# Expert products in unsplit fp32 on four 32-column groups of TensorE, instead of three split products on the whole array

## The chip, the core and the metric

The kernel runs on one core of a Trainium2 chip. The metric is the device time of one execution in microseconds (us). Below, PE is TensorE, ACT is ScalarE, DVE is VectorE, POOL is GpSimd and SP is SyncE, whose queue issues the weight loads.

## The reference

The program is a two-layer trunk for 256 tokens of 1024 numbers. Layer 0 is a gated mixer and a dense SwiGLU, layer 1 a gated recurrence (HGRN2) and a SwiGLU over experts. The change is in the experts:

```python
def swiglu(h, w_gu, w_down):
    gate, up = jnp.split(h @ w_gu, 2, axis=-1)
    return (jax.nn.silu(gate) * up) @ w_down

def moe_swiglu(h, w_router, b_router, w_gu, w_down):
    logits = (h @ w_router).astype(jnp.float32) + b_router.astype(jnp.float32)
    top_logit, top_idx = lax.top_k(logits, TOP_K)
    top_w = jax.nn.softmax(top_logit, axis=-1)
    gates = jnp.sum(jax.nn.one_hot(top_idx, N_EXPERTS, dtype=jnp.float32) * top_w[..., None], axis=-2)
    out = jnp.zeros_like(h)
    for e in range(N_EXPERTS):
        out = out + gates[..., e:e + 1] * swiglu(h, w_gu[e], w_down[e])
    return out
```

There are 8 experts, each token goes to 2 of them, and the inner width of an expert is 3584. All weights are fp32: 1024 x 7168 and 3584 x 1024 for each expert, 44 MB. For the inputs of this case the router sends 56, 64, 68, 53, 55, 73, 59 and 84 tokens to the eight experts.

## The kernel before

**Split products.** Every large product is made of three: a weight block W is split into `w_hi` (ACT, line 1075, a copy with rounding to fp32r) and `w_lo` (DVE, line 1487, W minus `w_hi`), the tokens likewise, and `split_matmul` (lines 508 to 510) adds hi x hi, lo x hi and hi x lo into one PSUM bank. A product takes 128 tokens as the stationary operand and 512 weight columns as the moving one.

**Weights.** They come in granules of 1 MB (128 partitions x 2048), each in two halves of 512 KB. A load lands in one of six places (three in `raw`, three in `SC`, which are free in the expert phase). ACT and DVE turn each half into a place of the rings `w_hi` and `w_lo`, six granules deep. SP waits for `lo_done` (DVE is done with the half) before it loads the place again, ACT waits for `used` (PE is done) before it fills a ring place again.

**The expert phase.** Work comes in items. An item is one expert with up to 128 of its tokens; an expert with more would get a further item. With the counts above there are 8 items. An item has seven units of 512 hidden columns. In a unit `unit_gu` makes the gate (`side` 0, bank 0) and the up part (`side` 1, bank 1), each 8 steps over the 1024 inputs, ACT applies silu (line 1375), DVE multiplies (line 1991), `unit_turn` transposes the 128 x 512 result in four pieces (line 963), ACT and DVE split it into `hT_hi` and `hT_lo`, and `unit_down` multiplies it with the down weights into banks 4 and 5, 8 steps. The order on PE is: gate and up of unit u+1, down of unit u, turn of unit u+1. A step below is one such piece of 128 inputs by 512 weight columns; a unit has 24 of them, an item 168, the phase 1344.

**Around an item.** The rows of the next expert's tokens are fetched by an indirect DMA (line 486), transposed by `turn_xg` (line 927) and split into `xT_hi`, `xT_lo`; an item's result is copied to `yo` (line 1383) and written to its tokens' rows by another indirect DMA (line 479). `turn_rows` (line 935) makes the row numbers. The last item isn't written out but stays as `ye` and is added with a selecting product (`scatter`, line 1047). The table of items is made by DVE (`tables`), in the middle of item 0. After the experts come the last norm and the gated embedding, again with split weights.

**Small fp32 products elsewhere.** Layer 1 has products that stay in fp32: `level` (lines 782 to 803) makes attention blocks whose stationary operand has 32 columns and whose output goes to PSUM partitions 0, 32, 64 and 96 in turn (line 794: only two of the four; line 787: 64 columns, one place).

Of the kernel before, what the change touches and what calls it, by code (L numbers as in the profile page):

```python
# [31 lines left out]
P = 128  # L32
# [11 lines left out]
def trunk(nc, x_d, pT_d, columns_d, norm_g, w_in_ab, a_ln_g, a_ln_b, wsT_d, w_out_ab, ffn_w_gu,  # L44
# [12 lines left out]
    XTRA = T * P * 2 // (P + 1)  # L57
# [15 lines left out]
    with ExitStack() as ctx:  # L73
# [15 lines left out]
        hT_lo = sb("hT_lo", [P, N], F32R)  # L89
        SC = sb("SC", [P, 9 * 1024 + 8])  # L90
# [19 lines left out]
        tab = sb("tab", [P, 2, T, ITEMS + 2])  # L110
        selT = sb("selT", [P, T, P])
# [33 lines left out]
        hh = junk[:, :].bitcast(F32)[:, N:2 * N]  # L145

# [29 lines left out]
        row = spare[:, 0:T * (ITEMS + 2)].rearrange("p (t j) -> p t j", t=T)  # L176
        dst = spare[:, 64:65].bitcast(I32)
# [8 lines left out]
        ye = raw[:, 0, 0:D].rearrange("p (k c) -> p k c", c=P)  # L186
# [41 lines left out]
        gat_done, xg_act, xg_ready = sem("gathered"), sem("xg_act"), sem("xg_ready")  # L228
        ye_act, sc_done, acc_done = sem("ye_act"), sem("scattered"), sem("acc_done")
# [64 lines left out]
        def _(sp):  # L294
            def load(g, src, turns=0, first=False):

                back = RAW if g < G_MOE or first else RING
                for s in range(2):
                    part = slice(s * HW, (s + 1) * HW)
                    if g >= RAW:  # L300
                        sp.wait_ge(lo_done, turns * 2 * RING + (2 * (g - back) + s + 1))
                    sp.dma_start(raw_part(g, s), src[:, part]).then_inc(raw_full[raw_slot(g)][s], 16)
# [61 lines left out]
            def unit_down(g, e, u, turns):  # L364
                for j in range(2):
                    src = dn[bass.ds(e, 1), bass.ds(u * (N * D) + j * 256 * D, 256 * D)]
                    load(g + j, src.rearrange("e (p m) -> p (e m)", p=P), turns)
# [35 lines left out]
        def _(pool):  # L403
# [37 lines left out]
            for n, v in enumerate(gains):  # L441
# [6 lines left out]
                pool.dma_start(gain[:, :], v.broadcast_to([P, D])).then_inc(gain_full, 16)  # L448
# [26 lines left out]
            def write_rows(i):  # L475
# [3 lines left out]
                pool.indirect_dma_start(ybuf[:, :], bass.IndirectOffsetOnAxis(ap=dst, axis=0), yo,  # L479
                                        None).then_inc(rows_written, 16)  # L480

            def fetch_rows(i):
# [3 lines left out]
                pool.indirect_dma_start(xg_rows, None, xbuf[:, :], bass.IndirectOffsetOnAxis(ap=origin, axis=0)).then_inc(x_rows, 16)  # L486
# [13 lines left out]
            pool.dma_start(xn[:, :, :], ybuf[SEQ:ROWS, :].rearrange("(t p) n -> p t n", p=P)).then_inc(y_loaded, 16)  # L500
            for t in range(T):
                root_y(3, t)
# [3 lines left out]
        def _(pe):  # L506
# [402 lines left out]
            def gather(quarter):  # L909

                for k in (2 * quarter, 2 * quarter + 1):
                    for t in range(T):
                        m = pe.matmul(PS[:, GATHERED[quarter], (k % 2) * P:(k % 2 + 1) * P], xn[:, t, k * P:(k + 1) * P],  # L913
                                      sel[:, t, :], start=(t == 0), stop=(t == T - 1), skip_group_check=True)
                m.then_inc(gat_done, 1)

            def turn_sel():
                for t in range(T):
                    m = pe.matmul(PS[:, 3, t * P:(t + 1) * P], sel16[:, t, :], ident16[:, :], start=True, stop=True,
# [3 lines left out]
            def turn_xg(n):  # L923

                pe.wait_ge(x_rows, n * 16)
                for k in range(KT):
                    m = pe.transpose(PS[:, 6 + k // HK, (k % HK) * P:(k % HK + 1) * P], xg_rows[:, k * P:(k + 1) * P], ident[:, :])  # L927
# [3 lines left out]
            def turn_rows():  # L931

                for t in range(T):
                    for a in range(2):
                        m = pe.matmul(PS[:, 3, 0:2], sel16[:, t, :], pick[:, t, a, :], start=(t == 0 and a == 0),
                                      stop=(t == T - 1 and a == 1), skip_group_check=True)
                m.then_inc(rows_psum, 1)

            def unit_gu(g, turns, tokens=None, sides=(0, 1), quarters=False):

                for side in sides:
                    for h in range(2):
                        if tokens is not None and side == 0:
                            pe.wait_ge(xg_ready, tokens + (h - 1))
                        for j in range(HK):
                            if quarters and j % 2 == 0:
                                pe.wait_ge(xg_ready, 2 * h + j // 2 + 1)
# [6 lines left out]
                            if j % 2:  # L954
                                m.then_inc(used, 1)

            def unit_turn(n):
                pe.wait_ge(h_ready, n)
                hv = hh.rearrange("p (j q r) -> p j r q", j=2, r=2)
                for j in range(2):  # L960
                    for r in range(2):
                        c = (j * 2 + r) * P
                        m = pe.transpose(PS[:, 2, c:c + P], hv[:, j, r, :], ident[:, :])  # L963
                m.then_inc(hT_psum, 1)

            def unit_down(g, n, last, turns, first=False):
                pe.wait_ge(hT_ready, n)
                for j in range(2):
                    for r in range(2):
                        pe.wait_ge(lo_done, turns * 2 * RING + (2 * (g + j) + r + 1))  # L970
                        for c in range(2):
                            a = slice((j * 2 + r) * P, (j * 2 + r + 1) * P)
                            w = slice(r * D + c * N, r * D + (c + 1) * N)
                            s = (g + j) % RING
                            m = split_matmul(PS[:, 4 + c, :], hT_hi[:, a], hT_lo[:, a],
# [1219 lines left out]
```

## Time and profile before

| | us |
|---|---|
| median of 3 runs (lowest to highest) | 1452.75 (1451.99 to 1452.84) |
| the profiled execution | 1452.55 |
| its span, first to last instruction | 1450.8 |

The span is 1.75 us shorter than the profiled execution's own time. An instruction's line is that of the helper that emits it, so the split products of all stages share lines 508 to 510, and the expert phase is found by its place in time.

### The profile page before, as it was taken

What the parts mean: (1) busy time and instruction counts of PE and PEld (TensorE: products, weight loads), DVE (VectorE), ACT (ScalarE), POOL (GpSimd) and SP (SyncE); (2) the same over time, 40 slices, a digit from 0 to 9 for tenths busy, and PEclk for the clock granted to TensorE, in tenths of its full rate; (3) what the DMA queues carried; (4) which work ended last, traced back from release to release, by engine and by line L of the source; (5) the groups of instructions that cost most, each with busy time, mean ns of one, the idle gap of its engine ahead of it and who ended that gap; (6) DMA issues with size and microseconds to landing.
All of it is one profiled execution on the core that took longest, in us unless ns stands there. A gap on an engine that the chain in (4) does not pass through costs nothing.

```text
span 1450.8 us, 24554 instructions
## 1 busy us (share of the span) xinstructions
PE 1440.7 (99%) x7475; PEld 1193.4 (82%) x7475; DVE 1215.0 (84%) x1439; ACT 1006.8 (69%) x1250; POOL 55.7 (4%) x60
## 2 busy tenths in 40 slices
PE   9999999999999999999999999999999999999998
PEld 6888888888787888888888888888888888888886
DVE  7986545567897999998898899999899989989985
ACT  7565444366357888777877787777787787778773
POOL 1010000000001300000000000000000000000000
PEclk9999999999999999999999999999999999999999
DMA  8577555466255999999999999999999989999960
GB/s 309 180 251 238 192 198 178 150 197 230 80 175 205 411 410 370 381 410 391 323 412 410 349 370 409 353 372 410 375 338 411 409 324 399 410 351 397 410 266 30
DMA packets 124786, 452.73 MB, mean 312 GB/s; under 512 B 14000, under 2 KB 14000, under 8 KB 124736
## 3 DMA queue, kind: packets, MB, share of 16 engines
q1 hardware_dynamic: 119952, 435.21, 79.7%
q0 software_dynamic: 4640, 16.82, 3.3%
q8 instruction: 31, 0.51, 0.1%
q14 instruction: 19, 0.16, 0.0%
q10 hardware_dynamic: 144, 0.03, 0.0%
HBM read 443.62 MB, written 8.39 MB: 312 GB/s over the span
## 4 chain that ended last, share of the span: by engine, by line
PE 97%; DVE 2%; issue 0%; DMA 0%; ACT 0%; SPq 0%; DVEq 0%
PE PS L508 30%; PE PS L510 30%; PE PS L509 30%; PE PS L963 2%; DVE w_lo L1487 1%; PE PS L559 1%; DMA raw<-in_w_in_ab 0%; PE PS L803 0%; PE PS L927 0%; PE PS L649 0%; PE PS L913 0%; PE PS L893 0%; PE PS L851 0%; PE PS L1047 0%; PE PS L769 0%
## 5 line engine op out<-in xcount | busy, mean ns | idle before, releaser
L1487 DVE TENSOR_TENSOR w_lo<-raw,w_hi 128x1024 fp32r<-128x1024 f32 x486 | 568.5, 1219 | 32.9 <-ACT w_hi L1075 30.5
L508 PE MATMUL PS<-w_hi,xT_hi 128*128 128x512 f32 x1432 | 567.7, 396 | 0.6 <-DVE w_lo L1487 0.6
L510 PE MATMUL PS<-w_lo,xT_hi 128*128 128x512 f32 x1432 | 558.2, 390 | 0.0
L509 PE MATMUL PS<-w_hi,xT_lo 128*128 128x512 f32 x1432 | 557.2, 389 | 0.0
L1075 ACT ACTIVATE w_hi<-raw 128x1024 fp32r<-128x1024 f32 x486 | 490.2, 1061 | 59.6 <-PE PS L510 38.1
L1487 DVE TENSOR_TENSOR w_lo<-SC,w_hi 128x1024 fp32r<-128x1024 f32 x340 | 392.1, 1218 | 8.0 <-ACT w_hi L1075 6.5
L1075 ACT ACTIVATE w_hi<-SC 128x1024 fp32r<-128x1024 f32 x340 | 336.9, 1061 | 17.1 <-DMA SC<-in_e_w_gu 6.9
L510 PEld LDWEIGHTS PS<-w_lo,xT_hi 128*128 128x128 f32 x1432 | 268.8, 188 | 57.2
L508 PEld LDWEIGHTS PS<-w_hi,xT_hi 128*128 128x128 f32 x1432 | 269.7, 188 | 54.0 <-issue 1.6
L509 PEld LDWEIGHTS PS<-w_hi,xT_lo 128*128 128x128 f32 x1432 | 269.3, 188 | 53.0 <-issue 0.2
L510 PE MATMUL PS<-w_lo,hT_hi 128*128 128x512 f32 x528 | 206.1, 390 | 0.0
L508 PE MATMUL PS<-w_hi,hT_hi 128*128 128x512 f32 x528 | 205.5, 389 | 0.0
L509 PE MATMUL PS<-w_hi,hT_lo 128*128 128x512 f32 x528 | 205.4, 389 | 0.0
L510 PEld LDWEIGHTS PS<-w_lo,hT_hi 128*128 128x128 f32 x528 | 99.1, 188 | 20.6
L508 PEld LDWEIGHTS PS<-w_hi,hT_hi 128*128 128x128 f32 x528 | 99.1, 188 | 20.5
L509 PEld LDWEIGHTS PS<-w_hi,hT_lo 128*128 128x128 f32 x528 | 99.1, 188 | 20.5
L1188 ACT ACTIVATE hT_hi<-PS 128x512 fp32r<-128x512 f32 x66 | 39.8, 603 | 87.3 <-PE PS L963 58.1
L1375 ACT ACTIVATE junk<-PS 128x512 f32<-128x512 f32 x56 | 33.5, 598 | 75.2 <-PE PS L510 75.2
L1699 DVE TENSOR_TENSOR hT_lo<-PS,hT_hi 128x512 fp32r<-128x512 f32 x66 | 45.4, 687 | 42.8 <-ACT hT_hi L1188 42.7
L1991 DVE TENSOR_TENSOR junk<-junk,PS 128x512 f32<-128x512 f32 x56 | 38.2, 683 | 24.3 <-ACT junk L1375 24.3
L1693 DVE SCALAR_TENSOR_TENSOR junk<-PS,lbc,junk 128x256 f32<-128x256 f32 x22 | 9.6, 479 | 39.1 <-ACT junk L1182 39.1
L486 POOL DMA_INDIRECT SC<-xbuf,seg x7 | 13.4, 1914 | 709.0 <-DVE seg L2064 709.0
(273 smaller groups left out, 592.7 us busy)
## 6 DMA issues: line engine op xcount, KB each, us to landing
raw<-in_e_w_gu SPq DMA_DIRECT2D x226, 512.0 KB, 9.3
SC<-in_e_w_gu SPq DMA_DIRECT2D x222, 512.0 KB, 9.0
SC<-in_e_w_down SPq DMA_DIRECT2D x114, 512.0 KB, 8.1
raw<-in_e_w_down SPq DMA_DIRECT2D x110, 512.0 KB
raw<-in_ffn_w_gu SPq DMA_DIRECT2D x44, 512.0 KB, 4.9
raw<-in_w_in_c SPq DMA_DIRECT2D x32, 512.0 KB, 6.2
raw<-in_ffn_w_down SPq DMA_DIRECT2D x22, 512.0 KB, 3.9
raw<-in_w_in_ab SPq DMA_DIRECT2D x20, 512.0 KB, 6.6
```

The costliest lines, as they stand in the source:

```text
L486: pool.indirect_dma_start(xg_rows, None, xbuf[:, :], bass.IndirectOffsetOnAxis(ap=origin, axis=0)).then_inc(x_rows, 16)
L508: pe.matmul(out, a_hi, b_hi, start=start, stop=False, skip_group_check=True)
L509: pe.matmul(out, a_lo, b_hi, start=False, stop=False, skip_group_check=True)
L510: return pe.matmul(out, a_hi, b_lo, start=False, stop=stop, skip_group_check=True)
L559: m = pe.transpose(PS[:, tile_bank(t, final) + b, j * P:(j + 1) * P], src[:, t, kt * P:(kt + 1) * P], ident[:, :])
L963: m = pe.transpose(PS[:, 2, c:c + P], hv[:, j, r, :], ident[:, :])
L1075: act.activation(w_hi[:, g % RING, part], raw_part(g, s), ACT.Copy).then_inc(hi_done, 1)
L1188: act.activation(hT_hi[:, :], PS[:, b, :], ACT.Copy).then_inc(hT_act, 1)
L1375: act.activation(sg, PS[:, 0, :], ACT.Silu).then_inc(silu_done, 1)
L1487: dve.tensor_tensor(w_lo[:, g % RING, part], raw_part(g, s), w_hi[:, g % RING, part].bitcast(F32), ALU.subtract).then_inc(lo_done, 1)
L1699: dve.tensor_tensor(hT_lo[:, :], PS[:, b, :], hT_hi[:, :].bitcast(F32), ALU.subtract).then_inc(hT_ready, 1)
L1991: dve.tensor_tensor(hh, sg, PS[:, 1, :], ALU.mult).then_inc(h_ready, 1)
```

## The change

The expert phase, and nothing before it, is rewritten.

1. Its products are plain fp32 on the weights where they landed (`raw_part`). `strips` makes one step out of six products with 32 stationary columns each. The 96 tokens of an item are three groups of 32. Group k's product with weight columns 0 to 383 goes to PSUM partitions 32k to 32k+31. Its product with columns 384 to 511 goes to partitions 96 to 127, at bank columns 128k on. So each of the four column groups of the array gets 384 weight columns in a step. An fp32 product is two passes, each with a weight load and a matmul instruction, as the trace of before shows for its own fp32 products.
2. An item holds 96 tokens (`CAP`), not 128. An expert could now need two further items; with the counts above there are still 8 items.
3. The splits of expert weights, of `xT` and of `hT` go away on ACT and DVE. silu and the product of gate and up run on 384 columns; the turn has three transposes, not four; ACT copies them to `he`; ACT and DVE copy half of the next tokens each to `xe`, which lies in the place of `gain`.
4. SP waits for `used` rather than `lo_done` before it loads an expert place again. PE waits for the landing (`raw_full`) rather than for `lo_done`.
5. `tables` runs before item 0; the gain of the last norm is loaded at the end of the experts; the weights of the last stage are split by `hi_tail` and `lo_tail` in the last item; the results are copied out in pieces (`output`, `ye_rest`).

```diff
+            def strips(bank, tokens, w, start, stop):
+
+                for k in range(CAP // 32):
+                    pe.matmul(PS[CAP:P, bank, k * P:(k + 1) * P], tokens[k], w[:, MAIN:N], start=start and k == 0, stop=stop,
+                              skip_group_check=True)
+                    m = pe.matmul(PS[32 * k:32 * (k + 1), bank, 0:MAIN], tokens[k], w[:, 0:MAIN], start=start, stop=stop,
+                                  skip_group_check=True)
+                return m
...
-                            if j % 2 == 0:
-                                pe.wait_ge(lo_done, turns * 2 * RING + (2 * (g + 2 * side + h) + j // 2 + 1))
-                            r = slice(j * N, (j + 1) * N)
-                            s = (g + 2 * side + h) % RING
-                            m = split_matmul(PS[:, side, :], xT_hi[:, HK * h + j, 0:P], xT_lo[:, HK * h + j, 0:P],
-                                             w_hi[:, s, r], w_lo[:, s, r], h == 0 and j == 0, h == 1 and j == HK - 1)
+                        if j % 2 == 0:
+                            landed(granule, j // 2, turns)
+                        m = strips(side, [xe[:, k, c:c + 32] for c in range(0, CAP, 32)],
+                                   raw_part(granule, j // 2)[:, j % 2 * N:(j % 2 + 1) * N], k == 0, k == KT - 1)
...
             def unit_turn(n):
                 pe.wait_ge(h_ready, n)
-                hv = hh.rearrange("p (j q r) -> p j r q", j=2, r=2)
-                for j in range(2):
-                    for r in range(2):
-                        c = (j * 2 + r) * P
-                        m = pe.transpose(PS[:, 2, c:c + P], hv[:, j, r, :], ident[:, :])
+                for b in range(3):
+                    m = pe.transpose(PS[:, 2, b * P:(b + 1) * P], hh[:, b * P:(b + 1) * P], ident[:, :])
                 m.then_inc(hT_psum, 1)
+
+            def down_round(g, j, r, c, start, stop):
+                b = 2 * j + r
+                if b < 3:
+                    tokens = [he[:, b * P + a:b * P + a + 32] for a in range(0, CAP, 32)]
+                else:
+                    tokens = [he[:, k * P + CAP:(k + 1) * P] for k in range(3)]
+                return strips(4 + c, tokens, raw_part(g + j, r)[:, c * N:(c + 1) * N], start, stop)
...
-                        sp.wait_ge(lo_done, turns * 2 * RING + (2 * (g - back) + s + 1))
+                        free = lo_done if g < G_MOE or first else used
+                        sp.wait_ge(free, turns * 2 * RING + (2 * (g - back) + s + 1))
...
             def unit_silu():
-                act.activation(sg, PS[:, 0, :], ACT.Silu).then_inc(silu_done, 1)
+                act.activation(sg[:, 0:MAIN], PS[:, 0, 0:MAIN], ACT.Silu).then_inc(silu_done, 1)
+
+            def unit_hT(n):
+                act.wait_ge(hT_psum, n)
+                act.activation(he[:, :], PS[:, 2, 0:MAIN], ACT.Copy).then_inc(hT_ready, 1)
...
+            next_rows(0)
+            tables()
+            item(0, False)
```

On PE, in the loop over the units of an item (the end of down, the turn), the program of before has, with `junk` the gated hidden block:

```order
L508 MATMUL PS<-w_hi,hT_hi 128x512
L509 MATMUL PS<-w_hi,hT_lo 128x512
L510 MATMUL PS<-w_lo,hT_hi 128x512
L963 MATMUL PS<-ident,junk 128x128 [waits h_ready]
L963 MATMUL PS<-ident,junk 128x128 x3
```

and the changed program has, at the same place:

```order
L959 MATMUL PS<-SC,he 32x128
L961 MATMUL PS<-SC,he 32x384
L959 MATMUL PS<-SC,he 32x128
L961 MATMUL PS<-SC,he 32x384
L959 MATMUL PS<-SC,he 32x128
L961 MATMUL PS<-SC,he 32x384
L988 MATMUL PS<-ident,junk 128x128 [waits h_ready]
L988 MATMUL PS<-ident,junk 128x128 x2
```

Three instructions of a step have become six, all on the landed weights (`SC` or `raw`), and the turn stands where it stood, with a transpose less. The last six rows before the turn are one step; each row is two passes.

On DVE, before the hidden product of a unit there stood six splits of expert weights, and four behind it:

```order
L1487 TENSOR_TENSOR w_lo<-raw,w_hi 128x1024 [waits hi_done]
L1990 REGISTER_ALU
L1991 TENSOR_TENSOR junk<-junk,PS 128x512 [waits silu_done]
L1486 REGISTER_ALU
L1487 TENSOR_TENSOR w_lo<-raw,w_hi 128x1024 [waits hi_done]
```

In the changed program the loop over units holds on DVE nothing but the hidden product:

```order
L2104 ISA
L2001 TENSOR_TENSOR junk<-junk,PS 128x384 [waits silu_done]
L2104 REGISTER_ALU
L2104 COMPARE_AND_BRANCH
```

So on DVE twelve splits a unit have gone, and PE no longer waits for DVE or ACT before it may use weights.

## Rows read from the trace of the kernel before

**Rows 1.** The page: busy time and share of the span.

```profile
PE 1440.7 (99%) x7475; PEld 1193.4 (82%) x7475; DVE 1215.0 (84%) x1439; ACT 1006.8 (69%) x1250; POOL 55.7 (4%) x60
```

**Rows 2.** Chain that ended last, expert phase: start us, us, what.

```profile
795.31 0.87 PE PS L927 x8
...
914.26 0.87 PE PS L927 x8
...
1372.73 0.47 PE PS L963 x4
1389.56 0.47 PE PS L963 x4
1406.40 0.47 PE PS L963 x4
```

**Rows 3.** Windows 460.30:1414.90 (expert phase), 676.30:795.30 (an item): busy us, clock, DMA share, GB/s.

```profile
460.30:1414.90 954.60, 953.66 (x4359) 792.75 (x4358) 878.63 (x946) 749.50 (x857) 32.66 (x17) 1.00 0.98 380
676.30:795.30 119.00, 119.00 (x547) 98.99 (x546) 108.76 (x115) 93.03 (x107) 3.09 (x2) 1.00 0.99 378
```

**Rows 4.** Timeline of PE at a turn and behind it: start us, us, engine.

```profile
1389.40 0.64 PE L963 MATMUL PS<-ident,junk 128*128 128x128 f32 x4
1389.79 0.47 PE L508 MATMUL PS<-w_hi,xT_hi 128*128 128x512 f32 x1
1390.11 0.39 PE L509 MATMUL PS<-w_hi,xT_lo 128*128 128x512 f32 x1
1390.33 0.39 PE L510 MATMUL PS<-w_lo,xT_hi 128*128 128x512 f32 x1
...
1391.26 0.39 PE L508 MATMUL PS<-w_hi,xT_hi 128*128 128x512 f32 x1
...
1400.10 0.39 PE L508 MATMUL PS<-w_hi,xT_hi 128*128 128x512 f32 x1
```

**Rows 5.** The chain again: plain fp32 products of 512 columns, and 128-column transposes.

```profile
1419.64 1.72 PE PS L1047 x4
1421.36 0.87 PE PS L559 x8
```

**Rows 6.** Timeline of PE around line 782, then 794, then 787.

```profile
365.17 0.39 PE L510 MATMUL PS<-w_lo,xT_hi 128*128 128x512 f32 x1
365.48 1.30 PE L782 MATMUL PS<-SC 128*32 128x32 f32 x128
366.71 0.51 PE L508 MATMUL PS<-w_hi,xT_hi 128*128 128x512 f32 x1
367.05 0.39 PE L509 MATMUL PS<-w_hi,xT_lo 128*128 128x512 f32 x1
394.08 1.21 PE L794 MATMUL PS<-SC 128*32 128x32 f32 x64
395.22 0.50 PE L508 MATMUL PS<-w_hi,xT_hi 128*128 128x512 f32 x1
398.16 2.08 PE L787 MATMUL PS<-SC 128*64 128x64 f32 x32
400.17 0.50 PE L508 MATMUL PS<-w_hi,xT_hi 128*128 128x512 f32 x1
```

**Rows 7.** Timeline of PE in the first block of line 803.

```profile
371.00 0.77 PE L803 MATMUL PS<-SC 128*32 128x16 f32 x69
372.43 0.69 PE L803 MATMUL PS<-SC 128*32 128x16 f32 x59 [0.66 <-issue]
```

**Rows 8.** The page and the DMA view of 640:676 us: queues, rates.

```profile
q8 instruction: 31, 0.51, 0.1%
DMA packets 4051, 14.75 MB, mean 410 GB/s; under 512 B 451, under 2 KB 451, under 8 KB 4051
```

**Rows 9.** Timeline of PE: a turn that had to wait, early in item 0.

```profile
489.36 0.74 PE L963 MATMUL PS<-ident,junk 128*128 128x128 f32 x4 [0.94 <-DVE junk L1991]
```

More of the change, by code:

```diff
@@ L365, in unit_down @@
                 for j in range(2):
-                    src = dn[bass.ds(e, 1), bass.ds(u * (N * D) + j * 256 * D, 256 * D)]
-                    load(g + j, src.rearrange("e (p m) -> p (e m)", p=P), turns)
+                    for s in range(2):
+                        src = dn[bass.ds(e, 1), bass.ds(u * (N * D) + (2 * j + s) * P * D, P * D)]
+                        sp.wait_ge(used, turns * 2 * RING + (2 * (g + j - RING) + s + 1))
+                        sp.dma_start(raw_part(g + j, s), src.rearrange("e (p m) -> p (e m)", p=P)).then_inc(
+                            raw_full[raw_slot(g + j)][s], 16)
             def load_item(i, e, following):
@@ L1425, in item @@
                 unit(EU - 2, None if last else True)
-                if not last:
-                    for q in (4, 5, 6):
-                        hi(G_MOE + ITEM + q, i * EU)
-            hi(G_MOE + 6)
             item(0, False, True)
@@ L1437, in _ @@
             ended = last_item * EU + EU
[L1438 removed]
+            for j in (1, 2, 3):
+                hi_tail(j, ended)
+            act.wait_ge(lo_done, 2 * G_MOE + 2)
             for c in range(2):
@@ L2015, in tables @@
-                step(dve.tensor_tensor(which, which, over.unsqueeze(1).broadcast_to([P, XTRA, E]), ALU.mult))
-                emit(dve.tensor_tensor(named, which, iota_c[:, 0:E].unsqueeze(1).broadcast_to([P, XTRA, E]), ALU.mult))
+                whiches = [rt[:, a:a + XTRA * E].rearrange("p (j e) -> p j e", j=XTRA) for a in (192, 128)]
+                which = whiches[0]
+                named = moved_at[:, 0:XTRA * E].rearrange("p (j e) -> p j e", j=XTRA)
+                moved = moved_at[:, 0:XTRA * T * E].rearrange("p (j t e) -> p j t e", j=XTRA, t=T)
@@ new lines, in tables @@
+                ordinal = [rt[:, 112 + k * XTRA:112 + (k + 1) * XTRA] for k in range(2)]
+                every = [P, XTRA, T, E]
+                for k in range(2):
+                    step(dve.tensor_tensor(pair, later, by_col(overs[k]), ALU.mult))
+                    step(dve.tensor_reduce(places[k], pair, AXX, ALU.add))
+                    step(dve.tensor_reduce(head[:, k:k + 1], overs[k], AXX, ALU.add))
+                step(dve.tensor_scalar(places[1], places[1], head[:, 0:1], None, ALU.add))
@@ L2090, in item @@
                     unit(u, False)
-                if first:
-                    tables()
                 if last:
@@ L2111, in _ @@
             item(last_item, True)
+            ended = last_item * EU + EU
+            for j in (1, 2, 3):
+                lo_tail(j)
+            dve.wait_ge(lo_done, 2 * G_MOE + 2)
+            for c in range(2):
+                if c == 0:
+                    dve.wait_ge(y_half, Y_MOE + 1)
+                else:
+                    dve.wait_ge(used, ended * 2 * RING + 2 * G_MOE)
+                for k in range(3):
+                    m = dve.tensor_copy(ye[32 * k:32 * (k + 1), c * N + MAIN:(c + 1) * N], PS[CAP:P, 4 + c, k * P:(k + 1) * P])
+                m.then_inc(ye_rest, 1)
             def add_acc(t):
```

267 lines of the change are left out of this document (123 added, 144 removed).

## The prediction

> **What bounds the kernel now.** I read the page first: PE is busy for 99% of the span, DVE for 84% [rows 1]. Busy is not yet bound, so the chain of waits comes next, and in the expert phase it is PE all along: the transposes of an item's tokens come back after 118.95 us, the turns of neighbouring units after 16.83 us, with nothing but split products between them [rows 2]. The phase lasts 954.6 us, at a granted clock of 1.00, which is 2.4 GHz [rows 3]. So its time is a count of PE steps times the length of one, and I price the change there. The timeline gives that length: 13 steps of three products lie between 1391.26 and 1400.10, so one takes 0.680 us, and 24 make 16.32 of a unit's 16.83 us; the turn and its surroundings are the other 0.51 [rows 2, 4]. A step's 3 x 512 columns at 2.4 GHz would be 0.640 us; each split product takes 13 ns more than its columns.
>
> DMA is the second thing to look at: it moved 380 GB/s in the phase, and 410 GB/s where it ran flat out [rows 3, 8]. An item's 44.04 MB at 410 GB/s take 107.4 us, with some 0.8 MB of token rows 109.4. That floor is 9.6 us under an item now.
>
> **The new step (the main term).** It is six fp32 products on groups of 32 columns. In the trace an fp32 product of 512 columns is two records of 0.430 us (four in 1.72), which is 1024 columns at 2.4 GHz, 0.427, and 3 ns; a 128-column record takes 0.109 (eight in 0.87) [rows 5]. So the fourth group, three products of 128 columns, needs 6 x 0.109 = 0.654 us a step, and each of the first three, 2 x 384 columns in each of two records, 2 x 0.323 = 0.646. If the groups run side by side, a step is 0.654 us.
>
> Do they? Line 782 is such a stream: 128 records of 32 columns, the four groups in turn, from 365.48 to 366.71, 1.23 us or 9.6 ns a record, though the two passes' 64 columns are 26.7 ns. Line 794 uses two groups in turn and needs 1.14 us for 64, 17.8 ns a record [rows 6]. So rate grows with groups, about 3 at a time for line 782, where the supply of instructions may already bound it: half as many columns on line 803 go no faster (59 records in 0.69 us, 12 ns each) [rows 7]. Here a record is ten times longer and supply matters less. Line 787, one place only, shows 2.01 us for 32 records, 63 ns against 53 of columns, 10 ns over [rows 6]. That is my upper bound on a record's cost on a part of the array: 6 x 0.117 = 0.700 us a step. The lower one is the first groups' 0.646. I take 0.654, since the records here are as long as those of rows 5 and the loads of 32 columns short.
>
> 1344 x (0.654 - 0.680) = **-35 us**; between -46 (0.646) and +27 (0.700).
>
> The Trainium skill ("TensorE: Matmul & The Clock Gate", Part 3, what overlaps and what doesn't) has matmuls start and end strictly in program order. By that rule the second pass of a product, which needs its own group, would hold back all behind it, and the step would be some 1.29 us. The trace doesn't agree: at line 782 a pair of passes would then take over 26.7 ns, and takes 19.
>
> **The other terms.**
> - *Turn.* 0.51 before. After: three transposes of 0.109 [rows 5] = 0.33; into column groups the first record comes 0.31 behind a split product instead of 0.23, +0.08; back to the whole array the second one comes 0.34 behind, +0.11 [rows 4, 6]. Sum 0.52: no change. ACT's copy to `he` has a gate and an up part, 10 us, to hide in.
> - *Groups that don't end together.* Before a turn the array must run empty. If only one product may wait for a busy group while later ones go past, the fourth group's products let the second and third group start 0.22 and 0.44 us late, and they end as late. If more may wait, nothing is lost. That happens at 56 turns and 8 `turn_rows` or `turn_sel`: 0 to 28 us. Rows 6 show that at least one is passed by, not how many; I take 0.1 each, **+6**.
> - *turn_rows* now interrupts a stream on groups: 8 x 0.2 = **+2**.
> - *Splits.* Twelve on DVE and twelve on ACT in a unit cost PE nothing, except where DVE came late, 0.94 us at the turn of 489.36 [rows 9]: **-1**. `tables` (some 40 operations of 0.2 us) lies now before item 0's second hidden product, which the turn needs only after a down of 5.2 us; its cover is thin, and if it's gone a few us are lost once.
> - *Loads.* A place is free when PE is done, not DVE. Eleven halves can be under way, 14 us of PE work, and a load lands in about 9. A unit now wants a half every 1.35 us on average, 390 GB/s: hidden, with 5% to spare.
> - *End.* The splits of the last weights end about when the last down does, and three copies to `ye` follow: **+1**.
> - *Instruction supply.* The built program's loop over items has 698 instructions on PE now, 2384 then. In the trace PE's code came in 31 packets of 16 KB [rows 8], some 260 instructions each for a program of 8066: each once, so loops of 698 stayed on the core. Where code was used up fast, PE once stood for 0.66 us [rows 7]. If the larger loop no longer stays, its five returns each wait so: 5 x 0.66 = **+3**, from 0 to 10 us.
>
> The Trainium skill ("Runtime: NRT & Kernel Launch", instruction fetch mechanics) gives PE room for 2048 instructions and says that a branch out of the resident part forces a fetch. By it the loop over items doesn't fit and that over units (590) does; the sum would be as it stands.
>
> Items stay eight, as no expert has over 96 tokens. Sum: -35 + 0 + 6 + 2 - 1 + 1 + 3 = -24. Against the profiled execution's 1452.55, 0.2 under the median, that is **1429 us**.
>
> **The rivals.**
> - *A, the forecast*: side by side, little lost at the turns. 1429, own range 1412 to 1445. Chance 0.50.
> - *B, one waiting product a group*: 28 us instead of 6, so 1451 (1440 to 1460). Rows 6 allow it. 0.17.
> - *C, a part of the array costs more per record*, or four streams hinder each other at the operands. At 0.700 a step: +27 + 11 = 1491. It decides from a step of 0.672 on, where the 24 us are gone. Line 787's 10 ns speak for it; that its weights are as wide as its columns, so that the load may set its rate, against it. This is the slower case, 0.20.
> - *D, strict order*: the fourth group's pass and the next one's take turns, 3 x (0.109 + 0.323) = 1.296 a step, 1344 x 0.616 = +828: about 2280. Lines 782 and 794 speak against it. 0.04.
> - *E, supply of instructions*: a step has 24 instructions for 6, so a packet lasts 7 us for 29. If each of some 9 packets an item costs 0.66, that is 8 x 6 = +48 - 3: 1474. Against it: at rows 7 PE used up a packet's worth in about a us, so the next could not be there; 7 us are another matter. 0.05.
> - *F, the loads*: 390 of 410 GB/s leaves little; if landings fall late PE waits, and an item costs 109.4 us at best but 118 or 119 with waits, so about 1453. 0.04.
>
> **How the numbers follow.** From no change the measurement can tell about 0.2%, 2.9 us. Faster holds nearly all of A (0.48), a third of B (0.06) and C's lower end (0.02), 0.56; same a part of B (0.07) and of F and A, 0.10; slower the rest of B and F, most of C, D and E, 0.34. The range is 1408 to 1492: below, A with 0.646 a step and no loss at turns; above, C. Outside lie D and a tail of A and C.
>
> **What would show it.** In the trace after, steps of groups: the start of one step's first record to the next's, 0.654 (A), 0.67 to 0.70 (C), 1.3 (D). Turns of neighbouring units lie 24 x 0.654 + 0.5 = 16.2 us apart (A), 16.6 (B). A gap of PE at the loops' edges with nothing that it waits for is E, an idle PE ended by a landing is F. The DMA rate in the phase should rise from 380 to about 390, ACT and DVE fall under a fifth busy there. I am wrong if a step is over 0.672.

## Result and the profile after

The changed kernel takes **1478.55 us** (median of 4 runs, 1477.36 to 1480.24), beside 1452.8 (1451.99 to 1453.34) for the kernel before in the same measurement: a ratio of 1.0179, 95% interval 1.0161 to 1.0196. It is slower by 1.8%. I had forecast 1429, range 1408 to 1492: the time lies in the range, on the other side of no change. The profiled execution took 1480.24 us, 1.7 above the median; its span is 1478.5.

The page and its DMA queues, beside [rows 1, 8]:

```profile
PE 1441.5 (98%) x19512; PEld 1310.0 (89%) x19515; DVE 399.3 (27%) x697; ACT 337.9 (23%) x570; POOL 38.5 (3%) x60
q8 instruction: 106, 1.74, 0.5%
```

DVE and ACT went from 84% and 69% to a quarter of the span, as meant. PE is busy as long as before, and its code comes in 106 packets where there were 31. The chain of waits, over two clean turns and then over the passage from item 1 to item 2, beside [rows 2]:

```profile
639.70 0.48 PE PS L988 x3
656.25 0.48 PE PS L988 x3
...
673.28 0.66 PE PS L943 x8
...
706.33 0.24 PE PS L961
706.57 4.84 issue
711.41 0.90 PE PS L988 x3
...
730.51 0.48 PE PS L988 x3
```

Clean turns are 16.55 us apart, where they were 16.83: the products did become shorter. Then PE stands for 4.84 us before a turn. "issue" says that it waited for no other engine and no load that the profile shows. What it does meanwhile is the branch back to the head of the loop over items (line 1067; PEldq is PE's sequencer; shortest, median and longest in ns, first and last start):

```profile
L1067 PEldq COMPARE_BRANCH  x6: 85/5935/6052, 705.2 to 1326.2; - x6
```

The first begins at 705.2 and takes 6.04 us. For 1.4 us of that PE still has products in its queue, then it stands. In the kernel before, the same branch takes 0.21 us (median 213 ns). The sixth, where the loop ends, goes straight on in 0.085 us.

The next unit takes 19.10 us from turn to turn, where the same unit without such a wait takes 17.15 (the second of the last item). PE's waits from 600 us to the end, as line, releaser, total us, times and longest:

```profile
PE PS L988 <- issue: 22.9, 5, 4.8
PE PS L1071 <- DVE raw L2133: 4.2, 1, 4.2
PE PS L524 <- DVE w_lo L2008: 0.3, 1, 0.3
```

Five times: once at each return of PE's loop over items 1 to 6. The windows tell what follows a return (us, busy time of PE, PEld, DVE, ACT and POOL, granted clock, DMA share, GB/s), beside [rows 3]:

```profile
690.00:706.00 16.00, 16.00 (x290) 15.83 (x291) 1.59 (x7) 0.98 (x2) 0.00 (x0) 1.00 1.02 390
706.00:712.00 6.00, 1.16 (x12) 0.56 (x4) 0.00 (x0) 1.94 (x4) 0.00 (x0) 0.93 0.96 385
711.40:716.00 4.60, 4.59 (x51) 3.92 (x53) 0.00 (x0) 0.49 (x1) 0.00 (x0) 0.65 0.11 43
716.00:719.00 3.00, 3.00 (x55) 2.56 (x48) 0.00 (x0) 0.00 (x0) 0.00 (x0) 1.00 0.77 235
730.50:747.00 16.50, 16.50 (x293) 15.90 (x292) 0.56 (x1) 0.98 (x2) 0.00 (x0) 1.00 1.03 409
```

Behind the 4.84 us the granted clock is 0.65 on average over 4.6 us, a mix of the two levels of 1.2 and 2.4 GHz, and 1.6 us of work are lost. Behind the second and the fifth wait PE runs at the lower level for the whole stretch (here the second), and these are the two longest of the units behind a return (20.20 and 20.29 in the table below):

```profile
835.30:840.00 4.70, 4.66 (x39) 3.79 (x41) 0.00 (x0) 0.49 (x1) 0.00 (x0) 0.50 0.10 37
```

The loads run on during the wait (385 GB/s), fill every place, and then nearly stop (43 GB/s) until PE frees one.

**Where the time went**, from turn to turn, against before:

| part | us |
|---|---|
| all 55 intervals between turns, at 16.55 for 16.83 | -15.2 |
| on top, 7 times each: `turn_xg` 0.66 for 0.87, `turn_rows` 0.60 for 0.24 | +1.1 |
| five returns: 21.46, 21.47, 21.33, 20.39, 21.38 for 16.55 | +23.3 |
| the units behind them: 19.03, 20.20, 19.17, 19.13, 20.29 for 17.15 | +12.1 |
| last turn to the end: 51.1 for 44.6 | +6.5 |
| sum; the span grew from 1450.8 to 1478.5 | +27.8; +27.7 |

The 19.10 above is from the wait's end, 19.03 from the turn's first transpose to the next one's; the other rows are read in the second way. Item 0's own differences, each of 0.5 us or less, nearly cancel and are left out.

The timeline of a clean turn (start us, length us), beside [rows 4]:

```profile
622.66 0.49 PE L961 MATMUL PS<-SC,he 128*32 128x384 f32 x1
623.07 0.55 PE L988 MATMUL PS<-ident,junk 128*128 128x128 f32 x3
623.55 0.30 PE L959 MATMUL PS<-SC,gain 128*32 128x128 f32 x1
623.56 0.52 PE L961 MATMUL PS<-SC,gain 128*32 128x384 f32 x2
623.68 0.38 PE L959 MATMUL PS<-SC,gain 128*32 128x128 f32 x2
623.80 0.51 PE L961 MATMUL PS<-SC,gain 128*32 128x384 f32 x1
```

Behind the turn the fourth group (L959) and two of the 384-column groups start within 0.01 us of each other; the third starts at 623.80, 0.24 later, when the fourth has finished two records of 0.11 and the queue can pass on. It ends as much later at the next turn.

### The profile page after: what moved, and what is told of

Its sections match the earlier page's. It is cut to its first block, busy times and chain, and to the rows that moved or that the text cites. A ratio compares the mean times of both kernels' runs of the same rounds, so it can differ in the third digit from the quotient of the medians.

```text
span 1478.5 us, 44860 instructions
## 1 busy us (share of the span) xinstructions
PE 1441.5 (98%) x19512; PEld 1310.0 (89%) x19515; DVE 399.3 (27%) x697; ACT 337.9 (23%) x570; POOL 38.5 (3%) x60
## 4 chain that ended last, share of the span: by engine, by line
PE 96%; issue 2%; DVE 1%; DMA 1%; ACT 0%; POOL 0%; POOLq 0%; DVEq 0%; ACTq 0%
PE PS L961 49%; PE PS L959 12%; PE PS L524 10%; PE PS L526 9%; PE PS L525 9%; PE PS L988 2%; PE PS L575 1%; DMA SC<-in_ple_w_gate 1%; PE PS L819 0%; PE PS L665 0%; PE PS L1071 0%; PE PS L943 0%; PE PS L593 0%; PE PS L929 0%; PE PS L909 0%
## 5 line engine op out<-in xcount | busy, mean ns | idle before, releaser
L961 PE MATMUL PS<-raw,gain 128*32 128x384 f32 x2712 | 325.3, 490 | 0.0
L961 PE MATMUL PS<-SC,gain 128*32 128x384 f32 x2664 | 322.3, 501 | 0.0
L959 PE MATMUL PS<-SC,gain 128*32 128x128 f32 x2664 | 309.5, 277 | 0.0
L959 PE MATMUL PS<-raw,gain 128*32 128x128 f32 x2712 | 306.6, 273 | 0.0
L959 PEld LDWEIGHTS PS<-SC,gain 128*32 128x32 f32 x2664 | 291.9, 112 | 12.0 <-issue 8.7
L959 PEld LDWEIGHTS PS<-raw,gain 128*32 128x32 f32 x2712 | 295.0, 110 | 1.7 <-issue 1.4
L524 PE MATMUL PS<-w_hi,xT_hi 128*128 128x512 f32 x536 | 213.6, 398 | 0.8 <-DVE w_lo L1504 0.5
L526 PE MATMUL PS<-w_lo,xT_hi 128*128 128x512 f32 x536 | 209.1, 390 | 0.0
L525 PE MATMUL PS<-w_hi,xT_lo 128*128 128x512 f32 x536 | 208.9, 390 | 0.0
L961 PEld LDWEIGHTS PS<-raw,gain 128*32 128x32 f32 x2712 | 207.3, 108 | 0.1
L961 PEld LDWEIGHTS PS<-SC,gain 128*32 128x32 f32 x2664 | 179.8, 109 | 0.0
L1504 DVE TENSOR_TENSOR w_lo<-raw,w_hi 128x1024 fp32r<-128x1024 f32 x144 | 168.9, 1221 | 23.2 <-ACT w_hi L1099 21.6
L959 PE MATMUL PS<-SC,he 128*32 128x128 f32 x1368 | 158.5, 273 | 0.0
L959 PE MATMUL PS<-raw,he 128*32 128x128 f32 x1320 | 153.3, 273 | 0.1
L1099 ACT ACTIVATE w_hi<-raw 128x1024 fp32r<-128x1024 f32 x144 | 145.3, 1063 | 29.2 <-PE PS L526 15.2
L959 PEld LDWEIGHTS PS<-SC,he 128*32 128x32 f32 x1368 | 149.3, 110 | 0.4 <-issue 0.4
L959 PEld LDWEIGHTS PS<-raw,he 128*32 128x32 f32 x1320 | 144.1, 110 | 0.0
```

The costliest lines, as they stand in the source:

```text
L524: pe.matmul(out, a_hi, b_hi, start=start, stop=False, skip_group_check=True)
L525: pe.matmul(out, a_lo, b_hi, start=False, stop=False, skip_group_check=True)
L526: return pe.matmul(out, a_hi, b_lo, start=False, stop=stop, skip_group_check=True)
L959: pe.matmul(PS[CAP:P, bank, k * P:(k + 1) * P], tokens[k], w[:, MAIN:N], start=start and k == 0, stop=stop, skip_group_check=True)
L961: m = pe.matmul(PS[32 * k:32 * (k + 1), bank, 0:MAIN], tokens[k], w[:, 0:MAIN], start=start, stop=stop, skip_group_check=True)
L1099: act.activation(w_hi[:, g % RING, part], raw_part(g, s), ACT.Copy).then_inc(hi_done, 1)
```

## The experiments

### Two first suspects of the five waits

**a_fit**: the turn of the next item's tokens ahead of the units, so that the unit written out behind the loop goes and PE's loop over items has 1797 instructions, not 2384.

```diff
-                with pe.Fori(1, EU - 2) as u:
-                    unit(u)
                 if not last:
                     turn_xg(i + 1)
-                unit(EU - 2)
+                with pe.Fori(1, EU - 1) as u:
+                    unit(u)
```

> The changed kernel with one edit: turn_xg stands before the loop over units and the loop takes the last unit too, so that the loop over items has 1794 instead of 2384 PE instructions. It still has the same edges and runs the same products. Theory 1 (the loop over items no longer stays on the core, each return waits for its code, and the packets behind it come late): the five PE waits of 4 to 5 us before a turn go, the units after them take 17.15 and not 19 to 20 us, the instruction packets fall from 106 to about 50, and the time falls by about 35 us, to 1443. Theory 2 (the loop's edge or the empty array costs this by itself with products on groups): the five waits stay and the time is 1478.

Measured: 1480.27 (1478.86 to 1484.46), ratio to before 1.0194 [1.0175, 1.0213]. The five waits stayed:

```profile
PE PS L988 <- issue: 24.9, 5, 5.2
```

Packets fell to 89 only, and item 0 now waits 3.0 us for the next item's token rows. So 1797 instructions are either still too many, or size isn't it. That was open until e_small and h_peeled.

### The step and the end

**b_mains**: in a step the three products of 384 columns go first, the three of 128 last.

```diff
                 for k in range(CAP // 32):
-                    pe.matmul(PS[CAP:P, bank, k * P:(k + 1) * P], tokens[k], w[:, MAIN:N], ...)
-                    m = pe.matmul(PS[32 * k:32 * (k + 1), bank, 0:MAIN], tokens[k], w[:, 0:MAIN], ...)
+                    pe.matmul(PS[32 * k:32 * (k + 1), bank, 0:MAIN], tokens[k], w[:, 0:MAIN], ...)
+                for k in range(CAP // 32):
+                    m = pe.matmul(PS[CAP:P, bank, k * P:(k + 1) * P], tokens[k], w[:, MAIN:N], ...)
```

> The changed kernel with one edit: in a step the three products of 384 columns are issued first, the three of 128 columns behind them. Theory 1 (at a turn the groups end up to 0.26 us apart because the third group's first product stands behind the fourth group's in the queue): the unit falls from 16.55 to about 16.3 us, 64 times 0.26 is 16 us, time 1462. Theory 2 (the 0.3 us above the turn's own price are the change of array form alone): the unit stays at 16.55, time 1478. Against both: if the fourth group's three products in a row block the others, a step gets longer than 0.655 us and the time rises.

Measured: 1464.91 (1463.21 to 1465.84), ratio 1.0079 [1.0062, 1.0096], 13.6 us under the changed kernel. Clean turns are 16.34 apart, 0.21 less than 16.55; over 56 units that is 11.8 us. The waits at the returns are unmoved (23.6 us, five times). The timeline in the middle of a down:

```profile
616.61 0.50 PE L959 MATMUL PS<-SC,he 128*32 128x384 f32 x3
616.83 0.27 PE L962 MATMUL PS<-SC,he 128*32 128x128 f32 x1
616.93 0.49 PE L959 MATMUL PS<-SC,he 128*32 128x384 f32 x2
...
617.25 0.49 PE L959 MATMUL PS<-SC,he 128*32 128x384 f32 x2
```

From one pass of the 384-column products to the next are 0.32 us, and the fourth group still needs six times 0.109: the step is still 0.655. What the order took away is the late start of a group behind a turn.

**c_tail**: ACT and DVE copy the last result to `ye` before they split the fourth granule of the last stage, whose load lands late, instead of behind it.

```diff
-            for j in (1, 2, 3):
+            for j in (1, 2):
                 hi_tail(j, ended)
...
                 act.activation(ye[0:CAP, c * N:c * N + MAIN], PS[0:CAP, 4 + c, 0:MAIN], ACT.Copy).then_inc(ye_act, 1)
+            hi_tail(3, ended)
```

(the same on DVE with `lo_tail`.)

> The changed kernel with one edit: the copies to ye stand before the splits of the third granule of the last gate weights on ACT and DVE, not behind them. Theory 1 (the end waits for splits queued ahead of ye, whose weights land late because a place is now freed by PE): the PE wait of 4.67 us before the first scatter falls to about 1, time 1475. Theory 2 (the last loads themselves bound the end, the split is needed right after): the wait moves to the first product of the last stage and the time stays.

Measured: 1474.03 (1472.08 to 1476.16), ratio 1.0141 [1.0124, 1.0158], 4.5 us under the changed kernel. The changed kernel's chain shows what it takes away:

```profile
1427.51 10.09 DMA SC<-in_ple_w_gate
1437.62 1.06 ACT w_hi L1404
1438.71 1.24 DVE w_lo L2008
...
1441.02 3.12 PE PS L1071 x4
```

PE's `scatter` (L1071) waited 4.2 us for copies that stood behind the split of weights that land at 1437.6. They land so late because their place is free only when PE, not DVE, is done with it: SP issues the last of these loads at 1434.6, 7 us behind the last turn, where before it did so at 1399.3, 7 us ahead of it. And the four products of `scatter` then take 3.12 us, for 1.81 before, at a granted clock of 0.60 (window 1441.00:1444.20). In c_tail the wait is 1.0 us.

**d_all**: the three edits together.

> All three edits together. If the three causes are apart and add: 1478.5 - 35 - 16 - 3.5 = 1424, which is under the kernel before (1452.8) by 2%. If only the code supply is a cause: 1443. If none is: 1478.

Measured: 1469.47 (1467.51 to 1471.82), ratio 1.0114 [1.0098, 1.0131]. It is 4.6 us slower than b_mains alone: a_fit brings its wait in item 0 (2.7 us), takes no return away, and the five waits are longer with it (26.3 us for 23.6).

### Size or edge

**e_small**: the text of a unit once in the loop over items, which has 1211 instructions on PE. An item's first unit is gate, up, down, turn, and the loop over units does the other six turns, the last of them already on the next item's tokens; ACT and DVE count every unit on the semaphores of the tokens, so that one wait fits all.

```diff
-                unit_turn(i * EU + (FB + 1))
-                if not first:
-                    unit_gu(G_MOE + 4, i * EU, None, (0,))
+                unit_gu(G_MOE + 4, i * EU, None, (0,))
+                if first:
+                    unit_turn(FB + 1)
...
-                with pe.Fori(1, EU - 2) as u:
-                    unit(u)
                 if not last:
                     turn_xg(i + 1)
-                unit(EU - 2)
+                with pe.Fori(1, EU - 1 if last else EU) as u:
+                    unit(u)
...
-                    unit_gu(G_MOE + ITEM - 2, i * EU, i + 3)
-                    unit_down(G_MOE + ITEM + 2, i * EU + (FB + EU), True, i * EU)
```

> The changed kernel with the unit's text written once in the loop over items: the first unit's gate and up, then the turn of the next item's tokens, then one loop over the other seven units. The loop over items shrinks from 2384 to 1211 PE instructions (before the change: 698; with the turn moved alone: 1794, and there the five waits stayed). Theory 1, the loop no longer fits in what PE keeps of its code: if 1211 fit, the five waits of 4.3 to 5.3 us at the returns go, the units behind them fall from 19 to 20 us to 17.2, the queue of PE's instructions shows some 60 packets and not 106, and some 35 us come back; item 0 waits about 3 us for its successor's token rows, as with the turn moved alone. Sum about 1447. Theory 2, the edge itself costs (the way back in the code or what stands at the edge, not its size): the five waits stay at 4 to 5 us, time 1475 to 1481. Packets as before the change but waits still there would refute theory 1 too.

Measured: 1445.16 (1443.35 to 1446.96), ratio **0.9944** [0.9928, 0.9959]: faster than before the change. The queue of PE's instructions, PE's only wait after 600 us, the branch back to the head of the loop over items, and the window 600:1300:

```profile
q8 instruction: 40, 0.66, 0.2%
PE PS L1066 <- DVE raw L2132: 2.1, 1, 2.1
L1062 PEldq COMPARE_BRANCH  x6: 82/213/215, 708.9 to 1294.7; - x6
600.00:1300.00 700.00, 700.00 (x12253) 672.67 (x12248) 35.71 (x112) 58.51 (x132) 12.00 (x13) 1.00 1.00 383
```

All five waits are gone, the branch takes 0.21 us, the clock is 1.00 throughout and the units that hold a return take 17.2 us. Item 0 pays: its second unit takes 20.93, not 16.56. Of that, 0.66 is `turn_xg`, which moved there, 1.9 the wait for the token rows, and most of the rest the clock behind it (0.89 over 485:500).

**h_peeled**: e_small with the last unit of items 0 to 6 written out behind the loop, 1803 instructions. What PE executes stays the same.

```diff
-                with pe.Fori(1, EU - 1 if last else EU) as u:
+                with pe.Fori(1, EU - 1) as u:
                     unit(u)
+                if not last:
+                    unit(EU - 1)
```

> The kernel with the unit's text once, but the last of the seven units of items 1 to 6 written out a second time behind the loop over units. What PE executes, its waits and its order are the same, instruction for instruction; only the loop over items grows from 1211 to 1803 PE instructions. If the size alone is the cause, the five waits of some 5 us and the slow units behind them come back, with about 90 packets of PE's instructions instead of 40: about 1445 + 32 = 1477. If it was something else in that rewriting (the place of the turn of the next tokens, the waits on its semaphores, the branch from the inner loop straight into the outer one), the time stays at 1443 to 1449.

Measured: 1481.11 (1479.2 to 1485.28), ratio 1.0191 [1.0174, 1.0208], **36 us** above e_small.

```profile
q8 instruction: 89, 1.46, 0.4%
PE PS L959 <- issue: 23.2, 5, 5.0
PE PS L1068 <- DVE raw L2134: 2.0, 1, 2.0
```

The five waits are back with the size alone, now one instruction group behind the turn (L959), where the loop's text begins. The branch takes 6.3 us again (median). The edge costs nothing by itself: in e_small the unit that holds it takes 17.18 us, and 17.15 where there is none.

### What a return costs, and in which form

**j_light**: the changed kernel with the gate and up transfers of the phase cut to a quarter of their columns (but for two granules of 28 an item, which stayed whole). The products read what the places held before, so its output isn't the reference's.

```diff
+                    if g < G_MOE + 4 or g >= G_MOE + ITEM:
                         sp.dma_start(raw_part(g, s), src[:, part])...
+                    else:
+                        sp.dma_start(raw_part(g, s)[:, 0:HW // 4], src[:, s * HW:s * HW + HW // 4])...
```

> The changed kernel, with each gate and up weight transfer of the expert phase cut to a quarter of its columns (the products read the whole place, whose other columns are old, so the output is not the reference's); the down weights are loaded whole. Bytes in the phase fall by half, the number of transfers, waits and instructions stays. It asks why a return costs 5 us where I had priced 0.66. If packets of instructions queue behind the weights' packets in the DMA engines, the five gaps shrink to 1 to 2 us and the units behind them to about 17.3: 1478 - 30 = about 1448. If the 5 us is the fetch's own latency, they stay at 4 to 5 us and only the slow units behind may change: 1466 to 1479. Clean units stay at 16.55 either way, since no load is waited for.

Measured: 1467.63 in one run.

```profile
PE PS L992 <- issue: 16.8, 5, 4.1
PE PS L1075 <- DVE raw L2137: 2.8, 1, 2.8
723.00:845.00 122.00, 119.09 (x2083) 114.02 (x2076) 6.04 (x19) 9.72 (x22) 1.84 (x2) 1.00 0.62 205
```

Over an item, 205 GB/s is little over half the bytes, and the waits sum to 16.8 us, not 22.9: 3.4 each for 4.6. The branch takes 4.4 us (median) for 5.9. But an item's average is not what the fetch meets. The transfers that stayed whole, the down weights above all, fall just into the returns; here the branch, and the window of the fourth wait:

```profile
L1071 PEldq COMPARE_BRANCH  x6: 85/4372/5329, 705.0 to 1317.1; - x6
1072.70:1075.80 3.10, 0.04 (x1) 0.00 (x0) 0.00 (x0) 1.94 (x4) 0.00 (x0) 1.00 0.88 303
```

During the five waits the rate is 283 to 357 GB/s and the DMA engines are 84 to 95% busy, where the changed kernel has 385 to 406 GB/s. So a lighter load makes the fetch shorter, by about 1.5 us here. How much of the remaining 4.4 us is still queueing and how much the fetch's own time, this run doesn't show; nor does it decide between my two expectations.

**k_before_long**: the kernel *before*, with PE's items in pairs and the inner units written out: a loop of 2372 instructions with two returns.

```diff
-            with pe.Fori(1, last_item) as i:
-                item(i, False)
+            with pe.Fori(0, 3) as v:
+                item(v * 2 + 1, False)
+                item(v * 2 + 2, False)
...
-                with pe.Fori(1, EU - 2) as u:
+                for u in range(1, EU - 2):
                     unit(u)
```

> The kernel before the change with PE's loops written out: items in pairs, the five inner units of an item one after the other. The loop then has 2372 instructions, as long as the changed kernel's, and two returns are left; what is executed is the same but for branches. Theory 1a, a loop that doesn't fit costs the same whatever it holds: two gaps of PE of about 5 us and slow units behind them, 1453 + 12 to 15 = about 1466. Theory 1b, the split form hides the fetch, because PE's queue holds more time in its larger instructions (0.227 us for each, where the column groups run six in 0.109): gaps of under 2 us, 1453 to 1457. Packets of PE's instructions rise from 31 to about 75 in either case.

Measured: 1460.0 (1458.8 to 1461.27), ratio 1.0053 [1.0037, 1.007].

```profile
q8 instruction: 63, 1.03, 0.3%
PE PS L963 <- issue: 4.2, 2, 2.2
831.40:836.00 4.60, 4.60 (x22) 3.89 (x23) 3.00 (x3) 3.89 (x5) 0.00 (x0) 1.00 0.62 247
1071.70:1076.00 4.30, 4.30 (x14) 3.48 (x15) 2.69 (x3) 3.58 (x5) 0.00 (x0) 0.60 0.56 224
```

The old form waits too, but 2.1 us a return, not 4.6. Behind the first return the clock stayed at 1.00 (the unit and its turn cost 2.3 us more), behind the second it fell to 0.60 (4.0 more). With its returns at 2.3 to 4.0 us it lies between my two expectations, nearer to the one in which the form hides part of the fetch. The trace shows that this is so. The branch, and the first wait in the chain:

```profile
L1043 PEldq COMPARE_BRANCH  x3: 83/5913/6063, 825.2 to 1307.3; - x3
829.36 1.98 issue
```

The branch takes 5.9 to 6.1 us in the old form as well. But PE reaches it at 825.2 and runs out of products only at 829.36: the work that is already queued covers 4.1 us of the branch, and the other 2.0 are the wait. In the new form it covers 1.4 us, and the wait is 4.8. So the branch takes both forms the same time; what differs is how much time the instructions that PE has already taken in are worth. A step of 0.66 us has 24 instructions in the new form, one of 0.68 us has 6 in the old.

**l_before_1559** and **m_before_1724**: the same pairs with inner loops, and one or two of the inner units of the pair's first item written out, for the bound of size.

```diff
+                for u in range(1, 1 + out):
+                    unit(u)
-                with pe.Fori(1, EU - 2) as u:
+                with pe.Fori(1 + out, EU - 2) as u:
                     unit(u)
```

> The kernel before the change with PE's items in pairs, and one inner unit of the first of them written out: a loop of 1559 instructions with two returns. 1211 stayed on PE and 1803 did not. If 1559 stays, packets of PE's instructions are 31 to 36, there are no gaps at the returns, and the time is 1452 to 1454. If not, packets rise to 45 or more and there are two gaps of 2.2 us as in the written out form of 2372: 1457 to 1460.

> As the run of 1559 instructions, with two inner units written out: a loop of 1724 instructions, which narrows the bound between 1559 and 1803. If it stays on PE: packets of PE's instructions 31 to 37, no gap at the two returns, 1452 to 1454. If not: packets 45 or more, two gaps of about 2 us, 1456 to 1460.

Measured, one run each: 1453.6 beside 1453.2, with 35 packets and no wait of PE after 600 us, for 1559; 1457.09 beside 1452.72 for 1724:

```profile
q8 instruction: 53, 0.87, 0.2%
PE PS L963 <- issue: 3.9, 2, 2.0
831.50:836.00 4.50, 4.49 (x22) 3.81 (x23) 2.83 (x3) 3.71 (x5) 0.00 (x0) 1.00 0.66 266
1071.60:1076.00 4.40, 4.40 (x21) 3.75 (x22) 2.75 (x3) 3.63 (x5) 0.00 (x0) 1.00 0.65 260
```

So 1559 stays and 1724 doesn't: the branch back takes 0.21 us with 1559 and 5.9 with 1724. Behind both waits of 1724 the clock stays at 1.00, and a return costs 2.2 us in all.

### The best version

**f_best**: e_small, b_mains and c_tail together.

> Three edits at once on the changed kernel: the unit's text once in the loop over items, the three products of 384 columns of a step ahead of the three of 128, and the copies of the last result ahead of the last late split. If the causes are apart and add: 1478.5 - 35 (code) - 14 (order of the step) - 4 (tail) + 3 (item 0's wait for token rows) = 1428, faster than before the change by 1.7%. Under theory 2 (the edge costs by itself) about 1463. If the five waits go but the time stays over 1440, then the products' own length has grown where the waits used to give the weights time to land: a wait for loads should then end PE's idle time in the units.

Measured: **1429.63** (1428.9 to 1433.31, 5 runs), ratio to before **0.9847** [0.9834, 0.9861].

```profile
PE 1413.0 (99%) x19512; PEld 1303.5 (91%) x19515; DVE 399.0 (28%) x697; ACT 338.0 (24%) x570; POOL 38.5 (3%) x60
560.00:1370.00 810.00, 810.00 (x14391) 790.85 (x14386) 44.25 (x133) 70.59 (x157) 13.48 (x15) 1.00 1.01 390
```

PE has not one wait in 810 us, at a full clock, while the loads run at 390 GB/s: clean units of 16.34 us, 17.0 and 16.74 around an item. The causes add: e_small's 33.4, b_mains' 13.6 and c_tail's 4.5 would give 1427.0.

**i_best2**: f_best with item 0's unit 1 written out ahead of the turn of item 1's tokens, outside the loop over items.

```diff
+                if first:
+                    unit(1)
                 if not last:
                     turn_xg(i + 1)
-                with pe.Fori(1, EU - 1 if last else EU) as u:
+                with pe.Fori(2 if first else 1, EU - 1 if last else EU) as u:
```

> The best version so far with unit 1 of item 0 written out ahead of the turn of item 1's tokens (in item 0's own text, so that the loop over items keeps its 1211 instructions). It removes item 0's wait for the token rows, 1.7 us at 487.8. If that wait was on the path, 1429.6 - 1.7 = 1428; if the loads take it over, 1429 to 1430.

Measured: 1430.66 (1430.52 to 1431.41), ratio 0.985 [0.9834, 0.9867]: no better. The wait in item 0 is gone (its units take 16.33 and 17.00, not 18.69 and 16.34), but the unit that leads into each of items 1 to 6, with `turn_rows` in it, takes 17.35 instead of 16.74, 3.7 us in all. The loop's text is the same and only its place in the program moved. What in that costs 0.6 us wasn't tried.

## Why the prediction was wrong

- **Bound, and the way to price it**: right. PE sets the phase before and after, and no load was waited for in a unit. At quarter gate and up transfers a clean unit is 16.55 us as well.
- **The new step**: right. I took 0.654 us; the fourth group's records follow at 0.109 and a step is 0.655, so -34 us for -35. The groups run side by side, and rivals C (0.700) and D (1.296) are refuted. My sign of being wrong, a step over 0.672, did not come: what turned the result lay outside the step.
- *Program order.* The Trainium skill ("TensorE: Matmul & The Clock Gate", Part 3, what overlaps and what doesn't) has matmuls start and end strictly in program order, by which a step would be near 1.29. The trace doesn't agree: it is 0.655.
- **Turn, and groups that don't end together**: a clean unit is 24 x 0.655 = 15.72 and 0.83 us. I had 0.52 and 0.1. The term of +6 was mis-sized: with the turn it is (0.83 - 0.51) x 56 = +18. Neighbouring turns are 16.55 apart, which is the sign I had named for B (16.6), not for A (16.2). But it is B's mechanism in part only: one group is late, by 0.24 us, about my 0.22 for the second one, and none by 0.44. b_mains takes 0.21 of it back, which leaves 0.62, as forecast. With the ends of the groups in line my two terms hold.
- **turn_rows, turn_xg, splits**: `turn_rows` came to +2.5 for +2. `turn_xg` is shorter on 96 tokens, -1.5, which I hadn't priced. Item 0's wait for DVE (0.94) is gone, as forecast.
- **End**: +1 was mis-sized; it is +6.5. I counted the copies to `ye` (0.3 each) but didn't ask behind what they are queued: a split that waits for a late landing, 4.2 us of waiting and 1.3 more in `scatter` at a low clock. c_tail gives 4.5 back.
- **Instruction supply: the step that failed.** "Its five returns each wait so: 5 x 0.66 = +3, from 0 to 10 us." The mechanism and its place were right, even the five returns; the price was too small, seven times for the wait (4.6 us) and eleven with what follows it. A return costs 3.8 to 4.9 us of wait and a further 1.9 to 3.1 in the next unit: +35.4 in all, more than the gain of the step. h_peeled against e_small shows it as 36.0 us from size alone. The 0.66 was from a place where the code runs straight on [rows 7]; a branch back to code that isn't there takes 5.9 us, of which the queued work hides 1.4. And I priced only the wait. The second part is the clock, at the lower level for part or all of the 4.7 us behind each wait. Rival E, with a chance of 0.05, had the size (+45) by another count: nine packets an item at 0.66. But the packets on straight code cost PE no wait that the trace shows; the time is lost at the returns alone. The sign that I named for E, a gap at the loops' edges, is what came.

That f_best comes to 1429.6 bears out the terms of the step and the turn (-34 and +6), not the whole sum: supply costs nothing there, and a longer end (48.3 us for 44.6) and item 0's wait of 1.5 us happen to stand in its place.

The Trainium skill ("Runtime: NRT & Kernel Launch", instruction fetch mechanics) gives PE room for 2048 instructions and says that a taken branch to code that isn't resident forces a fetch. The second part agrees (five branches of 5.0 to 6.1 us). The measured room is smaller: 1559 stayed, 1724 didn't. By the page's figure a_fit, at 1797, would have been enough, and it gave nothing.

**Open.** How long the fetch would take without load traffic: the branch took 5.9 us at about 400 GB/s and 4.4 at about 300, and no run had less. And the 0.6 us of i_best2.

## What to carry to other kernels

When a change multiplies the instructions of an engine, count the instructions of its outermost repeated loop, not only of the inner one. On PE a loop of 1559 came back free of charge and one of 1724 did not; then each return cost 2.2 to 4.0 us in the old form and 5.8 to 8.0 in the new one, wait and clock together. The finer the instructions, the less of a fetch the queued ones hide. Write a unit's text once, even if other engines must count a semaphore more often for it. Where column groups run side by side, order a step so that the long products of all groups come first, and ask of each copy at the end of a stage what it is queued behind. A shorter step can be real and still be lost at the edges: compare turn to turn before looking at sums.

## What the runs showed of the hardware

- PE's loops: 35 packets and no wait at 1559 instructions, 53 packets and two waits of 2.0 us at 1724, five of 4.6 us at 1803 in the new form. The bound lies between 1559 and 1724.
- PE's branch back takes 0.21 us when the loop stays and 5.9 to 6.3 us (medians) when it doesn't, in both forms. PE works off what is queued meanwhile: 1.4 us in the new form, 4.1 us in the old one.
- With 283 to 357 GB/s of loads instead of 385 to 406 the same branch took 4.4 us (median) instead of 5.9.
- Behind the five waits of 3.8 to 4.8 us the granted clock was 0.50 to 0.65 over the next 4.6 to 4.8 us. After four waits of 2.0 to 2.2 us it stayed at 1.00 three times and fell to 0.60 once.
- fp32 products on four column groups run fully side by side over 810 us (clock 1.00, 0.655 us for 6 products) while the loads bring 390 GB/s.
- A third group starts 0.24 us late behind a turn if the short products of a shared group stand between the long ones.
